# A two-layer decoder trunk: both layers in one unrolled program, four input tiles at a time

## The chip, the cores and the metric

The kernel runs on one core of one Trainium2 chip. The metric is the device time of one execution in microseconds (us); lower is better. Three runs of the kernel before gave 1854.80, 1850.37 and 1839.76 us, with a median of 1850.37 us. The engines are called PE (TensorE), ACT (ScalarE), DVE (VectorE), POOL (GpSimd) and SP (SyncE, which here only issues DMAs).

## The reference

A float32 decoder trunk with two layers, 512 tokens and a width of 1024. Cut to what matters here:

```python
for l in range(DEPTH):                       # DEPTH = 2
    h = rms_norm(x, norm_mix_pre[l])
    parts = jnp.split(h @ w_in[l], splits, axis=-1)
    # three head groups: latent attention (8 heads), mLSTM (4), dilated window attention (4)
    y = jnp.concatenate([y_a, y_b, y_c], axis=-1) @ w_out[l]
    x = x + rms_norm(y, norm_mix_post[l])
    h = rms_norm(x, norm_x_pre[l])           # cross-attention into 256 memory tokens
    y = memory_cross_attention(h, rms_norm(mem, norm_mem[l]), x_w_q[l], x_w_kv[l], x_w_o[l])
    x = x + rms_norm(y, norm_x_post[l])
    h = rms_norm(x, norm_ffn_pre[l])
    y = swiglu(h, w_gate_up[l], w_down[l])   # hidden width 2816
    x = x + rms_norm(y, norm_ffn_post[l])
```

## The kernel before

Everything is feature-major: `x` is 8 tiles of 128 features by 512 tokens and stays in SBUF. Each matrix product is split: operand and weight are each a high part (`h_hi`, `w_hi`) and a low remainder (`h_lo`, `w_lo`), and each 128 by 128 weight block costs three matmuls (lines 551 to 553, helper `three`).

**Weight stream.** The weights of a layer are 128 units of 512 KB, streamed in a fixed order through a ring of four slots (`RING`). For each unit SP loads `raw`, ACT copies it to `w_hi` (`split_unit`, line 852), POOL computes `w_lo` = raw - w_hi (`make_lo`, line 522), and PE uses both. SP may load a unit once the `w_lo` of the unit four before is made; ACT may write `w_hi` once PE has used the unit four before. POOL and SP walk through the units in hardware loops of four (`each_unit`).

**Layer loop.** The two layers are one hardware loop (line 488). Each turn is a block with one program for each engine, followed by a block that clears the semaphores, each with a meeting of all engines at its end. A block ahead of the loop loads `mem` (1 MB), the first gains, four weight units, `x` (2 MB) and the constants (1.7 MB), and makes the memory's `mem_rstd` (ACT square, 16 short matmuls at line 483, ACT Ln and Exp). The weights of units 0 to 3 come from a second array (`first_in`), and units 0 and 1 of the next layer are split ahead of the end of the loop's turn (`AHEAD` = 2). The last block stores `x` in one DMA of 2 MB (line 1499) and waits for it.

**Input stage** (lines 608 to 629 on PE). For each of the 8 k tiles of x, ACT makes `h_hi[k]` (`scaled_hi`) and the square `sq[k]` (two buffers), and DVE makes `h_lo[k]` (`scaled_lo`) and adds the square to `acc` (`add_square`). PE takes two output tiles side by side over k (m = 0 and 1, units 0 and 1), sums the squares over the partitions (`norm_sum`, line 596), and ACT turns the sum into `mix_rstd` (lines 873 and 875). Then come output tiles 2 to 9, one after the other, alternating between PSUM banks 0 and 1: tile m waits until tile m - 2 has been taken out by DVE (`take`, line 1134, multiplied by `mix_rstd`). After tile 7 PE waits for the squares of the query part (`norm_sum("q")`). `project_tokens` (96 matmuls, units 10 to 13) then fills banks 2 to 5 (`wide`), and the tile `sw` 0 follows. The 4-row matmuls at line 654 end the stage.

**DVE in that stage** (lines 1176 to 1242) has one fixed order: takes 0 to 9 in between the gates, four convolutions of four operations each (`convolve`), and four `silu` with a reciprocal of 3.35 us each. The take of tile 9 (`OG + 1`) stands at line 1224, ahead of the last `silu`, the norm of the query part and the taking out of the token-major banks.

**Residuals.** `residual` (line 1143) multiplies each y tile by `rstd` and adds it to x. After cross-attention and after the FFN, POOL adds tiles 1, 3, 4 and 6 (`POOL_ADDS`, line 528) and DVE the others; after cross-attention DVE makes `h_lo` and the square sums of the FFN's input in the same pass (`ffn_input`), and PE takes four gate/up tiles side by side over k.

## Time and profile before

| What | us |
|---|---|
| median of three runs | 1850.37 |
| lowest and highest run | 1839.76, 1854.80 |
| span of the profiled execution (first to last instruction) | 1837.1 |
| PE busy in it | 1674.5 (91%) |
| DVE busy | 1059.6 (58%) |
| ACT busy | 675.1 (37%) |
| POOL busy | 667.7 (36%) |

The span is taken in one profiled execution; the runs include what lies around it (the median is 13.3 us longer). Busy time of PE is modelled from pipelined matmuls, so a busy PE can still run below its peak; the column PEclk of a stretch is the TensorE clock that was granted (1.00 is 2.4 GHz, 0.50 is 1.2 GHz). A timeline row has its start, its length, engine, line and operation, and in brackets how long the engine was idle before it and what ended that.

### The profile page before, as it was taken

To read this page: it belongs to the slowest core of one execution; us is meant where nothing else is said; L and a number is where in the kernel's file an instruction comes from. 1 tells how busy PE (TensorE), PEld (TensorE's weight loads), DVE (VectorE), ACT (ScalarE), POOL (GpSimd) and SP (SyncE) were. 2 spreads that over 40 slices of the span, in tenths; PEclk is the share of its full clock that TensorE was granted. 3 is DMA by queue.
4 is the path that set the end of the run, shared out by engine and by line. 5 is a ranking of instruction groups with operands and counts; after the bars stand their busy time and mean duration, and the time that the engine had idled before them with its cause. 6 is when DMAs were issued, how large, how long until landed. Compare 5 with 4: busy or idle time off the path is not lost. (4 is left out here: it accounts for less than half of the span.)

```text
span 1837.1 us, 20577 instructions
## 1 busy us (share of the span) xinstructions
PE 1674.5 (91%) x7040; PEld 1267.2 (69%) x7040; DVE 1059.6 (58%) x1471; ACT 675.1 (37%) x1148; POOL 667.7 (36%) x280
## 2 busy tenths in 40 slices
PE   6998799989989999999769988998899899999994
PEld 4854456858667888888557545577677678888883
DVE  5977783661347786610279688727522587766003
ACT  5222574443442323322243226644343423232221
POOL 3321202563243444444333311035623345444442
PEclk9987899979989999999889889998999899999997
DMA  5211002332122232222122200023311132323231
GB/s 222 92 58 34 23 1 81 115 126 80 35 69 78 94 114 91 92 103 100 38 83 81 69 23 24 1 104 115 126 58 58 46 103 92 113 91 102 97 99 57
DMA packets 39100, 146.51 MB, mean 80 GB/s; under 512 B 4976, under 2 KB 4976, under 8 KB 38256
## 3 DMA queue, kind: packets, MB, share of 16 engines
q1 hardware_dynamic: 39024, 145.53, 23.4%
q8 instruction: 44, 0.72, 0.2%
q14 instruction: 32, 0.26, 0.0%
HBM read 143.41 MB, written 2.10 MB: 79 GB/s over the span
## 5 line engine op out<-in xcount | busy, mean ns | idle before, releaser
L522 POOL TENSOR_TENSOR w_lo<-raw,w_hi 128x1024 fp32r<-128x1024 f32 x252 | 620.6, 2469 | 1087.7 <-ACT w_hi L852 1087.6
L551 PE MATMUL bank<-h_hi,w_hi 128*128 128x512 f32 x1312 | 534.0, 407 | 69.8 <-DVE h_lo L1139 40.9
L552 PE MATMUL bank<-h_lo,w_hi 128*128 128x512 f32 x1312 | 520.0, 396 | 0.0
L553 PE MATMUL bank<-h_hi,w_lo 128*128 128x512 f32 x1312 | 519.6, 396 | 0.0
L551 PEld LDWEIGHTS bank<-h_hi,w_hi 128*128 128x128 f32 x1312 | 252.0, 192 | 144.2 <-issue 54.0
L852 ACT ACTIVATE w_hi<-raw 128x1024 fp32r<-128x1024 f32 x256 | 268.1, 1050 | 199.2 <-PE bank L553 199.0
L552 PEld LDWEIGHTS bank<-h_lo,w_hi 128*128 128x128 f32 x1312 | 252.4, 192 | 54.5 <-issue 3.2
L553 PEld LDWEIGHTS bank<-h_hi,w_lo 128*128 128x128 f32 x1312 | 251.9, 192 | 54.2
L1103 DVE TENSOR_TENSOR acc<-acc,sq 128x512 f32<-128x512 f32 x86 | 82.3, 956 | 321.7 <-ACT sq L864 320.0
L1455 DVE RECIPROCAL acc<-acc 128x512 f32<-128x512 f32 x44 | 147.5, 3353 | 1.5
L551 PE MATMUL bank<-a_hi,w_hi 128*128 128x512 f32 x352 | 138.7, 394 | 0.0
L553 PE MATMUL bank<-a_hi,w_lo 128*128 128x512 f32 x352 | 138.0, 392 | 0.0
L552 PE MATMUL bank<-a_lo,w_hi 128*128 128x512 f32 x352 | 136.6, 388 | 0.0
L1078 ACT ACTIVATE a_hi<-sq 128x512 f32 (+1 forms) x44 | 27.8, 632 | 253.2 <-DVE sq L1459 253.2
L864 ACT ACTIVATE sq<-bank 128x512 f32<-128x512 f32 x48 | 28.7, 598 | 147.0 <-PE bank L553 147.0
L553 PEld LDWEIGHTS bank<-a_hi,w_lo 128*128 128x128 f32 x352 | 66.1, 188 | 15.5
L552 PEld LDWEIGHTS bank<-a_lo,w_hi 128*128 128x128 f32 x352 | 66.1, 188 | 14.8
L551 PEld LDWEIGHTS bank<-a_hi,w_hi 128*128 128x128 f32 x352 | 66.2, 188 | 13.1
L1382 DVE CUSTOM_DVE_ANT_0 p_x<-bank,consts 128x256 f32<-128x256 f32 x32 | 13.6, 424 | 92.6 <-PE bank L783 91.6
L960 ACT ACTIVATE w_ml<-w_ml 128x512 f32<-128x512 f32 (+3 forms) x32 | 15.0, 470 | 135.6 <-DVE w_ml L1334 135.6
L1010 ACT ACTIVATE p_mix<-p_mix,stat 128x128 f32<-128x128 f32 (+1 forms) x96 | 53.6, 558 | 27.5 <-DVE stat L1382 27.4
L1382 DVE CUSTOM_DVE_ANT_0 p_mix<-bank,consts 128x128 f32<-128x128 f32 (+1 forms) x96 | 47.2, 491 | 21.2 <-PE bank L746 18.9
(184 smaller groups left out, 2212.8 us busy)
## 6 DMA issues: line engine op xcount, KB each, us to landing
raw<-w_in SPq DMA_DIRECT2D x248, 512.0 KB, 3.3
raw<-first_in SPq DMA_DIRECT2D x12, 512.0 KB, 3.5
mem<-mem_in SPq DMA_DIRECT2D x3, 1024.0 KB, 4.8
x<-x_in SPq DMA_DIRECT2D x1, 2048.0 KB, 10.6
out<-x SPq DMA_DIRECT2D x1, 2048.0 KB, 6.3
consts<-c_in SPq DMA_DIRECT2D x1, 1728.0 KB, 14.3
gains<-g_in SPq DMA_DIRECT2D x2, 36.0 KB, 4.1
first_g<-first_g_in SPq DMA_DIRECT2D x3, 4.0 KB, 3.3
```

The costliest lines, as they stand in the source:

```text
L522: pool.tensor_tensor(w_lo[:, s, :], raw[:, s, :], w_hi[:, s, :].bitcast(F32), ALU.subtract).then_inc(split_lo, 1)
L551: pe.matmul(out_ap, l_hi, r_hi, start=start, stop=False)
L552: pe.matmul(out_ap, l_hi, r_lo, start=False, stop=False)
L553: return pe.matmul(out_ap, l_lo, r_hi, start=False, stop=stop)
L852: act.activation(w_hi[:, s, :], raw[:, s, :], ACT.Copy)\
L864: act.activation(sq[:, c % 2, 0:width], src, ACT.Square).then_inc(squared, 1)
L960: act.activation(w_ml[:, u % 2, 0:n], w_ml[:, u % 2, 0:n], ACT.Exp).then_inc(ml_exp, 1)
L1010: act.activation(probs[:, u % PROBS, 0:n], probs[:, u % PROBS, 0:n], ACT.Exp, scale=-1.0, bias=stat[:, 0, u:u + 1], accum_out=stat[:, 1, u ...
L1078: act.activation(a_hi[:, bass.ds(j * (2 * SEQ) + i * SEQ, SEQ)], f_a[:, i, :], ACT.Copy)\
L1103: ins = dve.tensor_tensor(acc[:, :], acc[:, :], sq[:, s, :], ALU.add)
L1382: done(dve.tensor_tensor_reduce(probs[:, u % PROBS, 0:n], score_ring[u % 4][:, 0:n], const(mask(u // TB) + SEQ - n, n), -scale(u // TB), 3 ...
L1455: step(dve.reciprocal(e, e), 2)
```

## The change

- The layer loop, its barriers and the clearing of semaphores are gone: both layers are one unrolled program. Semaphores count on over both layers (`count`), waits are on constants; only the 10 turns of the gate/up loop stay hardware loops. SP and POOL are unrolled too.
- One weight array for 256 units; units 0 to 3 of the second layer are loaded and split as the ring gives room. All four are split before the second layer's input stage starts.
- At the start SP loads, in this order: unit 0, gains of both layers, x tiles 0 and 1, unit 1, x 2 and 3, unit 2, x 4 and 5, unit 3, x 6 and 7, constants. ACT splits unit k/2 ahead of x tile k. The memory's norm moves behind tile 5 of the first input stage; its data is loaded before unit 8.
- In the input stage PE takes four output tiles side by side over k (`HEAD` = 4); the ten output tiles go through banks 0 to 5 in turn (`IN_BANKS` = 6), and `project_tokens`, whose banks are 2 to 5, waits until DVE has taken out tile 9.
- The next layer's `h_hi`, `h_lo` and square sums are made inside the FFN's residual pass.
- All residual additions are on DVE.
- x is stored in four DMAs of 512 KB, each as soon as its two tiles are added.
- The memset of `ml_v` moves from before the first take to behind the query norm; the reload of `mem` is issued one unit earlier.

```diff
@@ sp, start and end
+                for s in range(RING):
+                    sp.dma_start(raw[:, s, :], w_in[s, :, :]).then_inc(raw_loaded[s], 16)
+                    if s == 0:
+                        sp.dma_start(gains[:, :, :], g_in).then_inc(gains_loaded, 16)
+                    sp.dma_start(x[:, 2 * s:2 * s + 2, :], x_in[:, 2 * s:2 * s + 2, :]).then_inc(x_loaded[s], 16)
+                sp.dma_start(consts[:, :], c_in).then_inc(consts_loaded, 16)
...
+                for i in range(KT // 2):
+                    sp.wait_ge(x_updated, count(x_updated, DEPTH - 1, N_SCALED - KT + 2 * i + 2))
+                    sp.dma_start(out[:, 2 * i:2 * i + 2, :], x[:, 2 * i:2 * i + 2, :]).then_inc(stored[i], 16)
@@ pe, project_step
-                        if k == 0 and use >= 2:
-                            wait_emptied(pe, use - 2)
+                        if name == "in" and k == 0 and m >= IN_BANKS:
+                            wait_emptied(pe, layer, use - IN_BANKS)
+                        if name != "in" and k == 0:
+                            wait_emptied(pe, layer, use - 2)
@@ pe, input stage
                     for k in range(KT):
                         after_norm("mix_pre")(k)
-                        for m in range(2):
+                        for m in range(HEAD):
                             project_step("in", m, k, tiles(h_hi), tiles(h_lo))
...
-                    for m in range(2, IN_FM):
+                    for m in range(HEAD, IN_FM):
                         project("in", m, tiles(h_hi), tiles(h_lo))
...
+                        if m == HEAD + 1 and layer == 0:
+
+                            pe.wait_ge(mem_squared, 1)
+                            pe.wait_ge(ln_done, 1)
+                            for k in range(KT):
+                                mm = pe.matmul(norm_bank[:, 0:N_MEM], const(C_ONES), mem_sq[:, k, :], start=(k == 0),
+                                               stop=(k == KT - 1))
+                            mm.then_inc(mem_summed, 1)
                         if m == ML[3]:
+                            if layer == 0:
+                                pe.wait_ge(mem_ln, 1)
                             norm_sum("q")
+                    wait_emptied(pe, layer, use_of("in", IN_FM - 1))
                     project_tokens(U_INV, wide, lambda k, b: h_hi[:, k, b * P:(b + 1) * P],
@@ act, before mix_rstd
                     for k in range(KT):
+                        if layer:
+                            wait_x(act, layer - 1, "ffn_post", k)
+                        elif k % 2 == 0:
+                            split_until(k // 2 + 1)
+                            act.wait_ge(x_loaded[k // 2], 16)
+                        scaled_hi(layer, k, G_MIX_PRE)
+                        square(layer, "mix_pre", k, x[:, k, :])
+                    split_until(HEAD + 1)
                     make_rstd("mix_pre", D_MODEL, mix_rstd)
@@ dve, residual and the end of the layer
-                                if name == "mix_post" or k - 1 not in POOL_ADDS:
-                                    dve.wait_ge(y_scaled, first + k)
-                                    done(dve.tensor_tensor(x[:, k - 1, :], x[:, k - 1, :], y[:, k - 1, :], ALU.add),
-                                         x_updated)
+                                dve.wait_ge(y_scaled, count(y_scaled, layer, first + k))
+                                done(dve.tensor_tensor(x[:, k - 1, :], x[:, k - 1, :], y[:, k - 1, :], ALU.add),
+                                     x_updated)
...
+                    def next_input(k):
+
+                        if k >= 1 and layer + 1 < DEPTH:
+                            scaled_lo(layer + 1, "mix_pre", k - 1, G_MIX_PRE)
+                            add_square(layer + 1, "mix_pre", k - 1)
+
+                    residual("ffn_post", "down", y_f, next_input)
+                    next_input(KT)
```

## Rows read from the trace of the kernel before

**Rows 1.** The page, parts 4 and 5: shares of the last chain; a costly group.

```profile
PE 36%; DVE 9%; issue 2%; ACT 1%; POOL 1%; DVEq 0%; POOLq 0%; ACTq 0%
...
L522 POOL TENSOR_TENSOR w_lo<-raw,w_hi 128x1024 fp32r<-128x1024 f32 x252 | 620.6, 2469 | 1087.7 <-ACT w_hi L852 1087.6
```

**Rows 2.** Busy time of each engine by stretch.

```profile
core 0: us, PE busy (x) PEld busy (x) DVE busy (x) ACT busy (x) POOL busy (x), PEclk, DMA share, GB/s
...
88.80:111.10 22.30, 22.30 (x98) 17.84 (x96) 17.82 (x19) 7.46 (x10) 10.94 (x4) 1.00 0.30 102
...
929.80:947.50 17.70, 14.17 (x50) 10.14 (x50) 15.57 (x17) 11.00 (x19) 5.69 (x2) 0.91 0.24 81
947.50:1000.90 53.40, 52.02 (x228) 42.02 (x229) 51.63 (x44) 17.49 (x24) 24.90 (x10) 1.00 0.28 94
```

**Rows 3.** Timeline, PE from layer 1 to layer 2 (start, length; idle before in brackets).

```profile
906.38 1.13 PE L596 MATMUL bank<-acc,consts 128*128 128x512 f32 x2 [1.48 <-DVE acc L1103]
...
929.84 0.79 PE L551 MATMUL bank<-h_hi,w_hi 128*128 128x512 f32 x1 [22.33 <-DVE h_lo L1139]
```

**Rows 4.** The page, part 6: DMA issues, count, KB each, us to landing.

```profile
raw<-w_in SPq DMA_DIRECT2D x248, 512.0 KB, 3.3
...
out<-x SPq DMA_DIRECT2D x1, 2048.0 KB, 6.3
consts<-c_in SPq DMA_DIRECT2D x1, 1728.0 KB, 14.3
```

**Rows 5.** Timeline, ACT, DVE and POOL as layer 1 starts.

```profile
23.15 1.04 ACT L852 ACTIVATE w_hi<-raw 128x1024 fp32r<-128x1024 f32 x1
...
24.10 0.71 ACT L884 ACTIVATE h_hi<-x,first_g 128x512 fp32r<-128x512 f32 x1
...
24.13 0.75 DVE L1139 SCALAR_TENSOR_TENSOR h_lo<-x,first_g,h_hi 128x512 fp32r<-128x512 f32 x1
...
24.27 2.86 POOL L522 TENSOR_TENSOR w_lo<-raw,w_hi 128x1024 fp32r<-128x1024 f32 x1 [10.98 <-ACT w_hi L852]
...
24.71 0.62 ACT L864 ACTIVATE sq<-x 128x512 f32<-128x512 f32 x1
...
24.92 2.77 DVE L1103 TENSOR_TENSOR acc<-acc,sq 128x512 f32<-128x512 f32 x1
```

**Rows 6.** Timeline, PE and DVE from cross-attention's residual into gate/up, layer 2.

```profile
1435.63 1.13 PE L596 MATMUL bank<-acc,consts 128*128 128x512 f32 x2 [1.48 <-DVE acc L1103]
1442.96 0.77 PE L551 MATMUL bank<-h_hi,w_hi 128*128 128x512 f32 x1 [6.20 <-DVE h_lo L1139]
...
1448.21 0.45 PE L551 MATMUL bank<-h_hi,w_hi 128*128 128x512 f32 x1
...
1456.02 0.69 DVE L1150 TENSOR_TENSOR y_x<-y_x,rstd 128x512 f32<-128x512 f32 x1
```

**Rows 7.** Timeline, layer 1: first input matmul, mix_rstd, end of the input stage.

```profile
17.72 0.50 PE L551 MATMUL bank<-h_hi,w_hi 128*128 128x512 f32 x1 [4.52 <-DVE h_lo L1139]
...
34.76 0.63 ACT L875 ACTIVATE mix_rstd<-mix_rstd 128x512 f32<-128x512 f32 x1
...
111.10 1.05 PE L654 MATMUL bank<-consts,gate 4*128 4x4 f32 x8
```

**Rows 8.** Timeline, input stage of layer 2: sum of squares, mix_rstd, DVE's chain.

```profile
945.03 1.10 PE L596 MATMUL bank<-acc,consts 128*128 128x512 f32 x2 [1.89 <-DVE acc L1103]
...
946.88 0.63 ACT L875 ACTIVATE mix_rstd<-mix_rstd 128x512 f32<-128x512 f32 x1
...
982.34 0.69 DVE L1103 TENSOR_TENSOR acc<-acc,sq 128x512 f32<-128x512 f32 x1
...
1000.24 0.69 DVE L1134 TENSOR_TENSOR o_gate<-bank,mix_rstd 128x512 f32<-128x512 f32 x1
```

**Rows 9.** Timeline, the end of the program.

```profile
1826.10 0.69 DVE L1155 TENSOR_TENSOR x<-x,y_f 128x512 f32<-128x512 f32 x1
1830.40 0.35 SPq L1499 DMA_DIRECT2D out<-x  x1
```

More of the change, by code:

```diff
@@ L224, in scaled_before @@
     return sum(k for n, k in NORMS[:NORM_AT[name]] if n in POST)
-def each_unit(eng, first, end, emit):
-    a, b = -(-first // RING) * RING, end // RING * RING
-    for n in range(first, min(a, end)):
-        emit(0, n)
-    if b > a:
-        with eng.Fori(a // RING, b // RING) as j:
-            for n in range(RING):
-                emit(j, n)
-    for n in range(max(a, b), end):
-        emit(0, n)
-def build(nc, x_in, mem_in, first_in, first_g_in, w_in, g_in, c_in, out):
+N_SQUARES = sum(k for _, k in NORMS)
@@ L280, in build @@
                 ml_qk = sb("ml_qk", [P, 4, SEQ], F32, early)
+                with ExitStack() as first:
+                    mem_sq = sb("mem_sq", [P, KT, N_MEM], F32, first)
                 ml_v = sb("ml_v", [P, TB, ML_HEADS, 2, ML_DK], F32, early)
@@ new lines, in _, with load @@
+                sp.dma_start(consts[:, :], c_in).then_inc(consts_loaded, 16)
+                def load(u):
+                    sp.wait_ge(split_lo, u + 1 - RING)
+                    sp.dma_start(raw[:, u % RING, :], w_in[u, :, :]).then_inc(raw_loaded[u % RING], 16)
+                for layer in range(DEPTH):
+                    first = layer * N_UNITS
+                    for n in range(0 if layer else RING, N_UNITS):
+                        if layer == 0 and n == 2 * RING:
+                            sp.dma_start(mem_sq[:, :, :], mem_in).then_inc(mem_first, 16)
+                        if n == U_OUT + RING + 1:
+                            sp.wait_ge(mix_at["out_lo"], count(mix_at["out_lo"], layer, MIX_HEADS))
+                            sp.dma_start(mem[:, :, :], mem_in).then_inc(mem_loaded, 16)
+                        load(first + n)
@@ L549, in three @@
+                pe.wait_ge(fixed_set, 2)
+                for layer in range(DEPTH):
                     def three(out_ap, l_hi, l_lo, r_hi, r_lo, start, stop):
@@ new lines, in _, with split_unit, split_to, scaled_hi @@
+            @block.scalar
+            def _(act):
+                done = counter(act)
+                act.preload_act_table_set("natural_log_exp_and_others")
+                made = [0]
+                def split_unit(layer, n, j=0):
+                    s = n % RING
+                    act.wait_ge(raw_loaded[s], j * 16 + count(raw_loaded[s], layer, 16 * (n // RING + 1)))
+                    if layer or n >= RING or not isinstance(j, int):
+                        act.wait_ge(unit_used, j * RING + count(unit_used, layer, n - RING + 1))
+                    act.activation(w_hi[:, s, :], raw[:, s, :], ACT.Copy).then_inc(split_hi, 1)
+                def split_to(layer, n):
+                    until = min(layer * N_UNITS + n, DEPTH * N_UNITS)
+                    while made[0] < until:
+                        split_unit(made[0] // N_UNITS, made[0] % N_UNITS)
+                        made[0] += 1
+                def scaled_hi(layer, k, g):
+                    act.activation(h_hi[:, k, :], x[:, k, :], ACT.Copy, scale=gains[:, layer, g + k:g + k + 1])\
+                       .then_inc(normed_hi, 1)
+                def square(layer, name, k, src, width=SEQ):
+                    c = layer * N_SQUARES + squares_before(name) + k
+                    if c >= 2:
+                        act.wait_ge(squares_added, c - 1)
+                    act.activation(sq[:, c % 2, 0:width], src, ACT.Square).then_inc(squared, 1)
+                for layer in range(DEPTH):
+                    def gain(col, rows=slice(0, P)):
+                        return gains[rows, layer, col:col + 1]
+                    def split_until(n):
+                        split_to(layer, n)
@@ L980, in _ @@
                         use = use_of("uk", m)
[L981 removed]
+                        wait_tile(act, layer, use)
                         for i in range(2):
@@ L1161, in tiles @@
                         return lambda k: t[:, k, :]
[L1164 to L1167 removed]
                     done(dve.memset(conv_in[:, :, 0:3], 0.0), pads_set)
[L1169 to L1171 removed]
+                    dve.wait_ge(rstd_ready, count(rstd_ready, layer, 1))
                     misc = c_tile(MISC)
```

598 lines of the change are left out of this document (248 added, 350 removed).

## Prediction

> **What bounds the kernel now.** I read the page's chain of waits first: PE has 36% of the chain that ended last, DVE 9% [rows 1], so PE is the bound where it has its operands and DVE where it hasn't. The table by stretch says where: in the token and `sw` part of the input stage PE is busy all 22.30 us with 98 matmuls, 0.2276 us each [rows 2]. That is PE's pace at full clock. Then I looked for places where PE has nothing: at the start (first input matmul at 17.72 [rows 7]), between the layers (idle for 22.33 us, ended by `h_lo` [rows 3]) and at the end (1826.79 to 1837.1). The change is aimed at these. Last I read DVE and POOL where PE is busy: in the 53.4 us behind the second layer's `mix_rstd` DVE is busy for 51.63 [rows 2]. PE and DVE are both full there, and the change ties them together anew.
>
> I call E the moment at which `mix_rstd` is ready: 34.76 + 0.63 = 35.39 in the first layer [rows 7], 946.88 + 0.63 = 947.51 in the second [rows 8]. The input stage ends at 111.10, 75.7 behind E [rows 7].
>
> **The store.** Before, the last addition ends at 1826.79, the store is issued at 1830.40 [rows 9] and takes 6.3 [rows 4]. After, DVE does eight scalings and eight additions of 0.69 each [rows 6, 9], about as long as now, when POOL's additions get in DVE's way. Only the last 512 KB lies behind them: a load of that size takes 3.3 [rows 4]. End: 1826.5 + 3.3 = 1829.8, that is **-7.3**. Bounds: a full 6.3 for the last piece, -4.3; 2.0 for it, -8.6.
>
> **Between the layers.** The new boundary has the form of the step from cross-attention to gate/up: residual with interleaved input, then four tiles over k. There PE's sum of squares starts at 1435.63, the first matmul at 1442.96, twelve matmuls run at half clock until 1448.21 (0.4375 each) [rows 6], and 84 at 0.2276 take 19.1: 1467.3. DVE needs 0.75 + 0.69 + 0.69 + 0.69 = 2.8 for each k [rows 5, 6, 9], PE 2.7, and DVE has a lead of 2.5, so DVE with all additions doesn't delay PE, here or after cross-attention, where I cost the moved additions at nothing. If that lead went, 8 x 0.1 is the price. From the sum's start to E it is 2.5 (945.03 to 947.51 [rows 8]): 1469.8, or 34.2 behind the start of the sum. After the FFN that sum starts at 906.38 [rows 3], so E = 940.6 instead of 947.5, **-6.9**. The fourth early split fits between two ACT operations; its `w_lo` falls on the first scaling, as it does after cross-attention. Bounds -5 and -9. Note how little 22 idle microseconds are worth: DVE needs four operations for each k where it had two passes, and PE does twice the matmuls before E.
>
> **The start of the first layer.** PE's first pass over m now needs four `w_lo` before it can go to k = 1. ACT splits in program order (w_hi 1.04, h_hi 0.71, sq 0.62; less where they overlap, 1.14 for a pair) [rows 5]; a `w_lo` is 2.4 on POOL alone (mean 2.469 [rows 1]). The row that matters is `acc` at 24.92: it took 2.77 instead of 0.69, because POOL worked from 24.27 to 27.13 [rows 5]; POOL in turn waited until `h_lo` ended at 24.88. So each `w_lo` stops DVE, and two square buffers make ACT wait for DVE. Worked out with the first landing at about 4 (0.7 + 3.3 [rows 4]) and the gains at 5.2:
> - w_hi 0 from 5.2 to 6.2, w_lo 0 to 8.7; h_lo 0 only then, to 9.3.
> - w_hi 1 behind k = 0 and 1, 8.4 to 9.5; w_lo 1 9.8 to 12.2; h_lo 1 and acc 1 to 13.6. sq 3 needs acc 1: 14.2.
> - w_hi 2 14.2 to 15.3; w_lo 2 15.9 to 18.3; acc 3 18.9. sq 5 needs acc 3: 19.5.
> - w_hi 3 19.5 to 20.6; w_lo 3 21.2 to 23.6.
>
> The DMAs aren't the gate: constants issued at 3.1 land at 17.4 behind 6.8 MB, and unit 3 is the first 3.7 MB [rows 4]. Behind PE's wait for w_lo 3 stand all matmuls of k = 1 to 7; ACT's split of unit 4 and `mix_rstd` wait for these. From 23.6 PE has 87 matmuls, 19.8, and 2.0 more at half clock: 45.4. With 2.5 more E = 48.0, **+12.6** though PE starts 8 us earlier. Bounds: with no blocking the chain is ACT's alone and w_lo 3 is ready at 18.5, +5.5 at full clock; with late gains and a slower first stretch, +15.
>
> The Trainium skill (SBUF — State Buffer, "Who interferes with whom" and the side section above it) says that the port pair of DVE and GpSimd is an exclusive lock held for a whole operation, not a split of bandwidth. By that rule the start costs the +12.6 above; were the pair shared, each `w_lo` would only stretch and the start would cost near +5.5. The trace agrees with the lock (2.77 for 0.69).
>
> **The input stage behind E.** Before, PE had tiles 2 to 9 left and its own banks for the tokens, so it never waited for the last takes. After, it has two tiles less to do, but `project_tokens` waits for take 9. That take ends at 1000.93, 53.4 behind E, and DVE had nearly no idle time before it: the chain of takes, convolutions and reciprocals is DVE's own and doesn't get shorter when PE is ahead. Behind PE's wait stand the tokens, the kv sum and `sw` 0, and DVE's taking out of the values and the mLSTM stage wait for those. Ten `w_lo` fall into it now (24.90 us of POOL [rows 2]), some eight after, since two are made earlier: I take 52.5. PE reaches `norm_sum("q")` at about E + 22 (E + 27 in the first layer, with the memory's norm) and waits for `acc`, ready at 983.03, E + 35.5 [rows 8]; tiles 8 and 9 with 12 slow matmuls take it to E + 50, within DVE's time. The tokens and `sw` 0 are 120 matmuls, 27.3, then the kv sum and the semaphore, 1.3: E + 81.1 instead of 75.7, **+5.4 in each layer**. The memory's norm in the first layer (5.4 of PE, 2.8 of ACT) lies in PE's wait for `acc` and costs nothing; without that cover 5.4. The `ml_v` memset (0.91) lies behind take 9 in DVE's slack while the tokens run. Bounds: 0 if DVE's blocking shrinks by 5, +8 if the tokens start at half clock.
>
> Barriers, clears and the first block are in the terms above. SP's earlier reload of `mem` meets a ring with three units made; 0.
>
> **Sum.** First layer +12.6 + 5.4 = +18.0; second -6.9 + 5.4 = -1.5; store -7.3: **+9.2**. Span 1837.1 + 9.2 = 1846.3, and the same added to the median, 1850.4 + 9.2 = 1859.6. I say 1859.
>
> **Rivals.**
> - *The new wait on take 9 doesn't bind.* DVE's chain is blocked less because PE's lead moves the `w_lo` under the reciprocals, which no row shows blocked. Then the term is 0 twice: +9.2 - 10.8 = -1.6, 1849. For: some 14 of the 53 us are blocking (the ten `w_lo` at 1.4 to 2.1 each, as the 2.08 of `acc` at the start [rows 5]). Against: the operations are the same, and ACT, which hands out the splits, still stops at the convolutions.
> - *Faster.* The same, and the start goes at ACT's pace (+5.5), and the chain shrinks until PE bounds it, -5 each: 5.5 - 10 - 6.9 - 7.3 = -18.7, 1832. It decides when take 9 ends before E + 43. The Trainium skill (Runtime: NRT & Kernel Launch, "Instruction fetch mechanics") says that a taken branch breaks the sequential fetch and that unrolling avoids this. By it this case would be likelier; but no row of POOL's idle time is ended by it, ACT's `w_hi` ends 1087.6 of 1087.7 [rows 1].
> - *Slower: the clock falls in the gap at `norm_sum("q")`* (8 to 14 us idle). If tiles 8 and 9 run wholly at half clock, 48 x 0.21 = 10 instead of 2.4 more, they end at E + 58, and the tokens start slow, +2.5. Against the sum each layer is 8.2 longer: +25.6, 1876. The gap before gate/up (6.20) cost twelve matmuls only, which speaks against; it decides from 4.7 more in each layer.
>
> **Chances.** Forecast 0.53 (own range 1851 to 1868), wait not binding 0.18, faster 0.09, slow clock 0.20. About 1% is what a measurement of this kernel can tell from no change: 1831.9 to 1868.9. The likeliest two lie inside; of the faster case most is just at the edge, of the slow case three quarters beyond, and of the forecast a little: faster 0.09, same 0.71, slower 0.20. The range leaves out the faster case and the far end of the slow one: 1840 to 1876.
>
> **What the changed profile would show.** The first four-tile round should complete not before 22, with `acc` or `h_lo` of 2.7 us beside each `w_lo`; E near 48 and near 958 (940.6 + 18.0 from the first layer); a wait of 8 to 14 us at the sum of the query squares and a wait of PE for DVE's take ahead of the tokens, which start 52 behind E; the sum after the FFN to the next E in 34; the last store 3.3 behind the last addition. I am wrong if the first round is complete by 18, if the tokens start before E + 48, or if the boundary takes longer than 37.

## The result and the profile after

The changed kernel takes 1847.78 us in the median (1844.44 to 1853.77, 20 runs) where the kernel before, in turn with it on the same chip, takes 1843.89 (1834.93 to 1854.80, 20 runs). The ratio is 1.0035, with a 95% interval from 1.0020 to 1.0049: 6.4 us more, 3.7 to 9.0 (the two medians alone differ by 3.9). A second comparison (`e14` below) gives 1.0027 [1.0012, 1.0041], 5.0 us more. The profiled execution has a span of 1851.4 us against 1837.1, that is 14.3 more; most of this section is about which part of the 14.3 is the change. Each run's time is 1.7 to 1.9 us above its own span, so the 13.3 us between span and median, which the section on the time before puts down to what lies around the span, are for the most part a difference between executions: a run of the kernel before with a span of 1837.1 has a time of 1838.9.

The page after, part 4 (the chain that ended last) and part 5 (costly groups: count, busy us, mean ns, idle before):

```profile
PE 75%; DVE 20%; ACT 2%; issue 1%; POOL 1%; DMA 0%; DVEq 0%; SPq 0%; ACTq 0%
...
L473 POOL TENSOR_TENSOR w_lo<-raw,w_hi 128x1024 fp32r<-128x1024 f32 x256 | 629.7, 2467 | 1178.3 <-ACT w_hi L804 1178.3
```

In [rows 1] the shares add up to 49%; here the chain is followed through the whole program, and PE and DVE hold 95% of it.

**The start.** Timeline of the changed kernel, PE, DVE, ACT and POOL (start, length; idle before in brackets):

```profile
8.72 0.76 PE L494 MATMUL bank<-h_hi,w_hi 128*128 128x512 f32 x1 [8.72 <-DVE h_lo L1092]
...
22.28 0.79 PE L494 MATMUL bank<-h_hi,w_hi 128*128 128x512 f32 x1 [4.92 <-POOL w_lo L473]
...
13.38 2.82 DVE L1086 TENSOR_TENSOR acc<-acc,sq 128x512 f32<-128x512 f32 x1
...
20.05 2.72 DVE L1086 TENSOR_TENSOR acc<-acc,sq 128x512 f32<-128x512 f32 x1
...
13.30 2.35 POOL L473 TENSOR_TENSOR w_lo<-raw,w_hi 128x1024 fp32r<-128x1024 f32 x1 [0.50 <-ACT w_hi L804]
19.40 2.82 POOL L473 TENSOR_TENSOR w_lo<-raw,w_hi 128x1024 fp32r<-128x1024 f32 x1 [3.75 <-ACT w_hi L804]
...
16.24 0.63 ACT L823 ACTIVATE sq<-x 128x512 f32<-128x512 f32 x1 [2.40 <-DVE acc L1086]
...
18.29 1.04 ACT L804 ACTIVATE w_hi<-raw 128x1024 fp32r<-128x1024 f32 x1
...
46.70 0.63 ACT L841 ACTIVATE mix_rstd<-mix_rstd 128x512 f32<-128x512 f32 x1
```

PE starts 9.0 us earlier than in [rows 7], and E (the moment at which `mix_rstd` is ready) comes 11.9 later (47.33 for 35.39). The fourth `w_lo` ends at 22.22, since POOL waited 3.75 us for ACT's `w_hi`, ACT's square had waited 2.40 for `acc`, and that `acc` took 2.82 instead of 0.69 beside the third `w_lo`.

**The input stage.** PE and DVE, first layer and then second:

```profile
84.17 2.04 PE L541 MATMUL bank<-acc,consts 128*128 128x512 f32 x2 [10.78 <-issue]
...
99.24 0.69 DVE L1137 TENSOR_TENSOR o_gate<-bank,mix_rstd 128x512 f32<-128x512 f32 x1
...
99.98 0.50 PE L494 MATMUL bank<-w_hi,h_hi 128*128 128x512 f32 x1 [1.17 <-DVE o_gate L1137]
...
993.70 2.08 PE L541 MATMUL bank<-acc,consts 128*128 128x512 f32 x2 [13.47 <-DVE acc L1086]
...
1009.23 0.50 PE L494 MATMUL bank<-w_hi,h_hi 128*128 128x512 f32 x1 [1.62 <-DVE o_gate L1137]
```

PE stands for 10.8 and 13.5 us at the sum of the query squares, and once more for the take of tile 9. The tokens start at E + 52.6 and E + 51.6 (before: 47.5 in both layers), and the stage ends at 128.29 and 1037.54, E + 81.0 and E + 79.9.

**Between the layers.** PE and ACT:

```profile
923.82 1.13 PE L541 MATMUL bank<-acc,consts 128*128 128x512 f32 x2 [1.48 <-DVE acc L1086]
...
930.89 0.77 PE L494 MATMUL bank<-h_hi,w_hi 128*128 128x512 f32 x1 [5.94 <-issue]
...
957.01 0.63 ACT L841 ACTIVATE mix_rstd<-mix_rstd 128x512 f32<-128x512 f32 x1
```

The 22.33 us of [rows 3] are 5.94, but from the sum to E it is 33.8 us where it was 41.1.

**The end.** The last two additions on DVE, and the DMA issues of the page's part 6:

```profile
1846.84 1.41 DVE L1150 TENSOR_TENSOR x<-x,y_f 128x512 f32<-128x512 f32 x2
...
out<-x SPq DMA_DIRECT2D x4, 512.0 KB, 2.6
```

The span ends at 1851.4, 3.1 behind the last addition; in [rows 9] it was 10.3.

**What a single profile hides.** The next table cuts the span of all profiled kernels at the sums of squares and at the matmuls that turn the gates. "Unchanged" is everything else: mLSTM, attention, cross-attention and FFN of both layers. There every kernel does the same work; what differs is that the unrolled kernels have no layer loop and no loops of units, that POOL or DVE makes four of the additions behind cross-attention, and where tensors lie.

| kernel | start to first sum | sum to gates, layer 1 | FFN's sum to next first sum | sum to gates, layer 2 | last sum to end | unchanged |
|---|---|---|---|---|---|---|
| before | 32.9 | 78.2 | 38.7 | 78.2 | 24.6 | 1584.5 |
| e6 (before, addresses) | 32.9 | 78.2 | 39.2 | 78.2 | 24.5 | 1597.9 |
| e13 (before, addresses) | 33.6 | 78.3 | 39.4 | 78.2 | 24.6 | 1585.0 |
| changed | 44.9 | 83.4 | 31.4 | 82.3 | 16.3 | 1593.1 |
| e14 (changed again) | 43.8 | 83.3 | 30.6 | 81.9 | 16.3 | 1591.9 |
| e4 (addresses, two more loads) | 46.5 | 83.6 | 31.5 | 82.3 | 16.3 | 1592.3 |
| e2 | 36.7 | 83.4 | 30.4 | 82.8 | 16.3 | 1585.4 |
| e1 | 27.1 | 86.6 | 30.7 | 81.9 | 16.3 | 1591.9 |
| e3 | 43.8 | 81.6 | 30.4 | 81.8 | 16.3 | 1587.1 |
| e10 | 44.8 | 79.6 | 30.6 | 79.8 | 16.3 | 1598.3 |
| e5 | 44.6 | 83.4 | 30.4 | 82.9 | 19.9 | 1586.3 |
| e8 (addresses) | 45.0 | 83.5 | 30.7 | 81.9 | 16.3 | 1585.1 |
| e7 | 26.3 | 81.2 | 25.5 | 78.0 | 16.3 | 1581.2 |
| e9 (e7, addresses) | 26.0 | 81.3 | 25.5 | 78.1 | 16.3 | 1590.9 |
| e11 (e7, addresses) | 26.9 | 81.2 | 25.5 | 78.1 | 16.3 | 1580.0 |
| e12 (e11, POOL adds) | 26.1 | 81.2 | 26.3 | 78.1 | 17.5 | 1576.9 |

The five changed stretches repeat within about 1 us in kernels that share their code. The unchanged ones don't: with the same code and the same addresses they took 1581 us (e7) to 1598 us (e10), at mean granted clocks of 0.968 and 0.953 in these stretches (0.966 and 0.948 over the whole execution). At equal clock the two programs can agree there to 0.1 us: from the gates to the next sum of squares, versions of the kernel before took 229.9, 233.2, 225.9 and 228.4 us at clocks of 0.911, 0.898, 0.917 and 0.918, and versions of the unrolled one 229.9, 233.1, 226.0 and 228.4 at the same four; other pairs with one mean clock still lie up to 2.9 us apart, in either program. Of the 14.3 us between the first two profiles, 8.5 lie in the unchanged part; 4.7 of them are the down projection (below), the rest is scatter of this kind. The changed stretches give +12.0 + 5.2 - 7.2 + 4.1 - 8.3 = +5.8 us for these two profiles; with means over three profiles of before and over the changed one, e14 and e8, it is +11.5 + 5.2 - 8.2 + 3.8 - 8.3 = +4.0.

### The profile page after: what moved, and what is told of

It is laid out like the page before. It is cut to its first block, busy times and chain, and to the rows that moved or that the text cites. A ratio compares the mean times of both kernels' runs of the same rounds, so it can differ in the third digit from the quotient of the medians.

```text
span 1851.4 us, 19318 instructions
## 1 busy us (share of the span) xinstructions
PE 1687.9 (91%) x7040; PEld 1273.8 (69%) x7040; DVE 1054.8 (57%) x1486; ACT 671.2 (36%) x1144; POOL 635.9 (34%) x262
## 4 chain that ended last, share of the span: by engine, by line
PE 75%; DVE 20%; ACT 2%; issue 1%; POOL 1%; DMA 0%; DVEq 0%; SPq 0%; ACTq 0%
PE bank L494 21%; PE bank L495 20%; PE bank L496 20%; PE bank L709 3%; PE bank L703 3%; PE bank L681 2%; DVE tn_x L1120 2%; DVE x L1150 2%; PE bank L750 2%; DVE y_x L1146 2%; PE bank L740 1%; DVE ml_qk L1174 1%; DVE conv_in L1183 1%; PE bank L633 1%; DVE o_gate L1297 1%
## 5 line engine op out<-in xcount | busy, mean ns | idle before, releaser
L473 POOL TENSOR_TENSOR w_lo<-raw,w_hi 128x1024 fp32r<-128x1024 f32 x256 | 629.7, 2467 | 1178.3 <-ACT w_hi L804 1178.3
L1086 DVE TENSOR_TENSOR acc<-acc,sq 128x512 f32<-128x512 f32 x86 | 74.7, 868 | 327.3 <-ACT sq L823 325.6
L1371 DVE CUSTOM_DVE_ANT_0 p_x<-bank,consts 128x256 f32<-128x256 f32 x32 | 13.6, 425 | 94.3 <-PE bank L740 93.3
```

The lines of the kernel that those rows point to most:

```text
L473: pool.tensor_tensor(w_lo[:, u % RING, :], raw[:, u % RING, :], w_hi[:, u % RING, :].bitcast(F32), ALU.subtract).then_inc(split_lo, 1)
L1086: ins = dve.tensor_tensor(acc[:, :], acc[:, :], sq[:, c % 2, :], ALU.add)
L1371: done(dve.tensor_tensor_reduce(probs[:, u % PROBS, 0:n], score_ring[u % 4][:, 0:n], const(mask(u // TB) + SEQ - n, n), -scale(u // TB), 3 ...
```

## The experiments

My theory was that of the prediction: the loss is the first layer's four tiles and the tokens' wait for the last take; the gains are the boundary and the store. The ratios below are to the kernel before on the same chip; "against the changed kernel" means against 1.0031, the mean of its two ratios, at 1841 us. Each ratio is uncertain by 0.15 to 0.3%, 3 to 6 us.

### Two tiles in the first layer (e1)

```diff
+        def head(layer):
+            return HEAD if layer else 2
-                        for m in range(HEAD):
+                        for m in range(head(layer)):
```

> The first layer takes two input tiles at a time over k again, the second layer still four. Theory (the first layer's loss lies in the first pass of PE over m, which needs four w_lo, each of them tied behind DVE and ACT): the first pair needs only the first two w_lo, complete at about 13 us, the pass over k then takes as long as before the change (17.7 us), mix_rstd is ready at 29 to 31 us instead of 47.3, the input stage ends at 110 to 113 instead of 128.3, and the kernel is 16 to 18 us faster than the changed kernel, 1830 to 1832. Rival A (cold unrolled code or the first weights' landing sets the start whatever the number of tiles): mix_rstd stays after 40, gain under 7. Rival B (the start is regained, but given back behind mix_rstd, since PE has two more tiles to do there): mix_rstd at 30 but the input stage ends after 118, gain under 10.

1833.16 us, ratio 0.9958 [0.9937, 0.9978]: 13 us faster than the changed kernel. ACT and PE of its first layer:

```profile
28.90 0.63 ACT L845 ACTIVATE mix_rstd<-mix_rstd 128x512 f32<-128x512 f32 x1
...
83.45 0.80 PE L498 MATMUL bank<-w_hi,h_hi 128*128 128x512 f32 x1 [5.89 <-DVE o_gate L1141]
...
113.72 1.05 PE L615 MATMUL bank<-consts,gate 4*128 4x4 f32 x8
```

E comes at 29.53, 17.8 earlier; the stage ends 14.6 earlier, at E + 84.2, because PE waits 5.9 us for the take of tile 9, which ends at E + 53.9. The theory holds for the start; 3 us go the way of rival B, and the gain of 13 us lies below the 16 to 18 expected.

### Weights ahead of x (e2)

```diff
-                            split_until(k // 2 + 1)
+                            split_until(RING)
```

and the loads of x stand behind those of the four units.

> The four first weight units are loaded ahead of x, and ACT rounds all four before it touches x; four tiles over k stay. Theory (the fourth w_lo is late because ACT rounds units 1 to 3 only between squares that wait for acc on DVE, which each w_lo on POOL stops): the fourth w_lo ends at 15 to 17 us instead of 22.2, mix_rstd is ready at 39 to 42 instead of 47.3, and the kernel is 5 to 8 us faster than the changed kernel. Rival (POOL's own work or the landing of the units is the bound): the fourth w_lo stays after 20 and the gain is under 2 us.

1838.99 us, ratio 0.9986 [0.9965, 1.0007]: 8 us faster than the changed kernel. POOL and ACT:

```profile
5.66 9.90 POOL L474 TENSOR_TENSOR w_lo<-raw,w_hi 128x1024 fp32r<-128x1024 f32 x4 [5.21 <-ACT w_hi L805]
...
38.52 0.63 ACT L842 ACTIVATE mix_rstd<-mix_rstd 128x512 f32<-128x512 f32 x1
```

The four `w_lo` are made in 9.9 us without a break (DVE's first operation beside them starts at 12.21, during the third) and end at 15.56, 6.7 earlier; E at 39.15 is 8.2 earlier. e2 moves the loads too, but these were not what made the fourth late: in the changed kernel unit 3 had landed at 13.68 us, and ACT came to split it at 18.29. It was the interlocking of ACT, POOL and DVE.

### The wait for the last take (e3, e10)

e3 puts tiles 8 and 9 into banks 0 and 1 and the query's sum behind tile 9; e10 keeps the sum, and after the first four tiles uses banks 0 and 1 only, as before the change:

```diff
-                    wait_emptied(pe, layer, use_of("in", IN_FM - 1))
+                    wait_emptied(pe, layer, use_of("in", HEAD - 1))
```

> Input tiles 8 and 9 go to the two banks of the later tiles, so that the six banks of the tokens are free once DVE has taken tile 5; the sum of the query squares moves behind tile 9. Theory (PE's wait for the take of tile 9 sets the input stage's end): the tokens start about E + 45 or earlier instead of E + 52.6, the stage ends at E + 73 to E + 76 instead of E + 81.0 and E + 79.9, and the kernel is 9 to 15 us faster than the changed kernel. Rival (DVE's chain is the bound anyway, and the mLSTM stage waits for DVE instead): the tokens start earlier, but the stage's end moves by under 2 us in each layer, and so does the kernel.

> The changed kernel, four tiles over k in banks 0 to 3, but the later tiles alternate in banks 0 and 1 as before the change, so that the tokens have banks 2 to 5 for themselves and don't wait for the take of tile 9; the sum of the query squares stays where it is. Theory (the wait on the last take makes the input stage longer, by its place in PE's order and not by DVE's chain): the tokens start between E + 46 and E + 49, the stage ends at E + 75.5 to E + 77.5 in both layers instead of E + 81.0 and E + 79.9, mix_rstd as in the changed kernel (47.3), and the kernel is 6 to 9 us faster than the changed kernel. Rival (DVE's chain of takes bounds it in any case, as with the sum moved): E + 79 or more, gain under 3.

e3 takes 1846.13 us, 1.0028 [1.0005, 1.0051]; e10 1846.08, 1.0021 [1.0002, 1.0041]. PE in the first layer of e3, then of e10:

```profile
83.72 0.80 PE L494 MATMUL bank<-h_hi,w_hi 128*128 128x512 f32 x1 [11.44 <-DVE q_mla L1136]
...
96.81 0.80 PE L494 MATMUL bank<-w_hi,h_hi 128*128 128x512 f32 x1
...
125.40 1.05 PE L610 MATMUL bank<-consts,gate 4*128 4x4 f32 x8
```

```profile
71.31 0.79 PE L494 MATMUL bank<-h_hi,w_hi 128*128 128x512 f32 x1 [5.86 <-DVE q_mla L1137]
...
96.13 0.39 PE L494 MATMUL bank<-w_hi,h_hi 128*128 128x512 f32 x1
...
124.31 1.05 PE L611 MATMUL bank<-consts,gate 4*128 4x4 f32 x8
```

In e3 (E = 46.22) the wait for take 9 is gone, but one of 11.4 us for take 6 (the `q_mla` of the row) stands in its place at tile 8, after it PE starts slowly (0.80 for a matmul), and the tokens start at E + 50.6. The stage ends at E + 79.2: 1.8 gained, 0.5 in the second layer. The expectation of 9 to 15 us was wrong. In e10 (E = 47.16) the waits come earlier and the tokens start at E + 49.0, the stage ends at E + 77.2 and E + 77.4, that is 3.8 and 2.5 earlier. Take 9 itself ends later in e10, at E + 54.4; it was the place of the wait in PE's order, and not DVE's chain, that cost these us. The stretches are as e10's theory had them, 6.3 us in sum; its gain of 6 to 9 us in the kernel's time is not shown: the ratio gives 2 with 3.6 of uncertainty, and this profile had the slowest unchanged part of all.

### One store at the end (e5)

```diff
-                for i in range(KT // 2):
-                    sp.wait_ge(x_updated, count(x_updated, DEPTH - 1, N_SCALED - KT + 2 * i + 2))
+                sp.wait_ge(x_updated, count(x_updated, DEPTH - 1, N_SCALED))
+                sp.dma_start(out, x[:, :, :]).then_inc(stored[0], 16)
```

> The four stores of 512 KB become one of 2 MB behind the last addition. Theory (the store's term of the prediction): the last DMA takes 6.3 us to landing instead of 2.6, so the kernel is 3.7 us slower than the changed kernel, 1851 to 1852. Rival (the pieces share the same queues and the last one is not faster for being small, or the end is set elsewhere): less than 1 us of difference.

1852.10 us, ratio 1.0055 [1.0034, 1.0076]: 4.4 slower than the changed kernel; the last stretch is 19.9 instead of 16.3. Part 6 of its page gives the one transfer as:

```profile
out<-x SPq DMA_DIRECT2D x1, 2048.0 KB, 6.3
```

### The input stage of the kernel before, in the changed program (e7)

```diff
-HEAD = 4
-IN_BANKS = 6
+HEAD = 2
+IN_BANKS = 2
-                    wait_emptied(pe, layer, use_of("in", IN_FM - 1))
```

and the first sum stands behind the last k of tile 0, as before the change.

> The changed kernel (one program without barriers, one weight stream, pieces of the store, additions on DVE) with the input stage of the kernel before: two tiles over k in both layers, two banks for the input tiles, and the tokens in banks of their own, without the wait for the last take. Theory (four tiles and six banks cost more than they give in both layers, the rest of the change gains): mix_rstd is ready at 29 to 31 us in the first layer and 30 to 34 behind the sum after the FFN in the second; each input stage ends 75 to 77 behind mix_rstd, instead of 81.0 and 79.9; the kernel is 21 to 27 us faster than the changed kernel, 1820 to 1826, and faster than before by over 0.8%. Rival (at the boundary four tiles are what hides DVE's four operations for each k): mix_rstd of the second layer comes no later than with four tiles only if PE catches up; if it comes over 37 behind the sum, the gain is that of the first layer alone, 14 to 18.

1816.49 us, ratio 0.9878 [0.9848, 0.9908]: 22 us faster than before and 28 faster than the changed kernel. Its chain, ACT at both E's, and the table by stretch for the boundary and the second input stage:

```profile
PE 77%; DVE 18%; ACT 2%; issue 1%; DMA 0%; POOL 0%; DVEq 0%; SPq 0%; ACTq 0%
```

```profile
28.16 0.63 ACT L841 ACTIVATE mix_rstd<-mix_rstd 128x512 f32<-128x512 f32 x1
...
925.35 0.63 ACT L841 ACTIVATE mix_rstd<-mix_rstd 128x512 f32<-128x512 f32 x1
```

```profile
core 0: us, PE busy (x) PEld busy (x) DVE busy (x) ACT busy (x) POOL busy (x), PEclk, DMA share, GB/s
...
898.00:926.00 28.00, 16.29 (x52) 9.98 (x52) 22.04 (x33) 13.28 (x22) 2.35 (x1) 0.88 0.07 20
926.00:1001.60 75.60, 74.38 (x325) 59.95 (x325) 70.37 (x64) 24.96 (x32) 36.20 (x14) 1.00 0.30 97
```

The boundary takes 28.0 us from the sum to E, though PE is busy for only 16.3 of it: DVE's pace for each k sets it, and two tiles are done by then. One `h_lo` follows the other after 2.84 us, and PE waits 1.2 of them for it. With four tiles, 96 matmuls in place of 48 stand ahead of E. The second stage takes 75.6, as before the change, and PE is busy for 74.4 of it: nothing is lost by doing the two tiles there. The first takes 78.7, 3.1 more than the second, where the memory's norm is missing: it now has no wait of PE to hide in (its matmuls run from 41.8 to 45.1). E and the boundary come slightly earlier than expected, and so the kernel is faster than the 1820 to 1826 asked for. Against the means of the kernel before the stretches of the table give -6.8 + 3.0 - 13.6 - 0.2 - 8.3 = -25.9, and the down projection +4.7: -21, where the ratio says 22 (17 to 28).

### The pace of the down projection (e4, e6, e8, e9, e11, e13)

The traces showed a difference that my sum doesn't contain. PE in the down projection, first and last of a run of back-to-back matmuls; before (36 of them), changed (36), e8 (37):

```profile
849.80 0.39 PE L551 MATMUL bank<-a_hi,w_hi 128*128 128x512 f32 x1
...
857.81 0.39 PE L553 MATMUL bank<-a_hi,w_lo 128*128 128x512 f32 x1
```

```profile
849.61 0.39 PE L495 MATMUL bank<-a_lo,w_hi 128*128 128x512 f32 x1
...
857.77 0.40 PE L494 MATMUL bank<-a_hi,w_hi 128*128 128x512 f32 x1
```

```profile
849.74 0.39 PE L496 MATMUL bank<-a_lo,w_hi 128*128 128x512 f32 x1
...
857.90 0.39 PE L496 MATMUL bank<-a_lo,w_hi 128*128 128x512 f32 x1
```

8.01 / 35 = 0.2289 us from start to start before, 8.16 / 35 = 0.2331 in the changed kernel, 8.16 / 36 = 0.2267 in e8, all at a granted clock of 1.00 and with no wait between them. The code is the same; what differs is where the tensors lie. The changed kernel has gains of 640 bytes for each partition where there were 320 in two tensors, and a `stat` of 576 bytes instead of 768. Over all 528 matmuls of a layer the first and the last start are 120.6 us apart before, 123.0 in the changed kernel and 119.5 in e8, the same in both layers. The edits move small tensors only (e4 also loads the gains in three pieces), for example in e8:

```diff
-        stat = sb("stat", [P, 3, MIX_UNITS])
+        stat = sb("stat", [P, 2, MIX_UNITS])
+        sb("gap", [P, 16])
```

> The changed kernel with the gains in three tensors, so that the weight ring, y_f, h_hi, h_lo and sq stand at the SBUF addresses that they have in the kernel before (in the changed kernel they lie 320 bytes higher); a_hi and a_lo stay at the changed kernel's addresses (128 bytes higher). Nothing else differs but two small loads more at the start. The matmuls of the down projection go at one each 0.2334 us in the changed kernel and 0.2289 in the one before. Theory A (the address of the ring does it): 0.2289 here, the FFN stage 1.1 to 3 us shorter in each layer, the kernel 2 to 5 us faster than the changed kernel. Theory B (the address of a_hi and a_lo, or something that is no address): 0.2333, no difference above 1 us.

> The kernel before, with 320 unused bytes behind the gains and 192 bytes less in stat, so that ring, h_hi, h_lo, a_hi and a_lo stand at the changed kernel's addresses; no instruction differs but in addresses. If SBUF addresses set the pace of the down projection, its matmuls go at 0.2333 us here instead of 0.2289, and the kernel is 2 to 5 us slower than before. If they don't (the unrolled program or its waits do), it is 0.2289 and within 1 us of before.

> The changed kernel with a_hi and a_lo 128 bytes lower, at the addresses that they have in the kernel before (stat keeps two rows instead of three, and the reciprocal overwrites the row of the maxima); ring, h_hi and h_lo stay where the changed kernel has them. Theory A, now that the ring alone didn't bring the pace back and the kernel before lost it with both moved: the address of a_hi and a_lo sets the pace of the down projection, so its matmuls go at 0.2289 us each instead of 0.2333, the stretch from the sum ahead of gate/up to the one behind down is 1.5 to 2.5 us shorter in each layer, and the kernel is 3 to 5 us faster than the changed kernel (1842 to 1845 where the kernel before takes 1841). Theory B (ring and a must both stand as before): 0.2333 and no gain.

> The version with two tiles and own banks (e7), all tensors from x on 32 bytes up and a_hi and a_lo 160 bytes down, so that ring, h_hi, h_lo, a_hi and a_lo begin at multiples of 64 bytes; before, in the changed kernel and in e7 they all begin 32 bytes beside one. If a multiple of 64 is what matmul's moving operand wants, down goes faster than 0.2289, gate/up faster than in e7, and the kernel is 5 us or more faster than e7 (under 1812). If only the distance of the address from something else counts, down goes at 0.2289 or 0.2333 and the kernel stays within 4 us of e7 (1812 to 1818).

> e7 (two tiles, own banks) with a_hi and a_lo left at the changed kernel's address, and ring, h_hi and h_lo 128 bytes up, so that the distance from the ring to a_hi is a multiple of 256 bytes, as it was in e8 (down at 0.2267 us each) and in none of the others (rest 64 in the kernel before: 0.2289; rest 128 in the changed kernel, 192 in the two others: 0.2333). Theory A (the distance between the weights and the moving operand, modulo 256 bytes, sets the pace): 0.2267, the stretch from the sum ahead of gate/up to the one behind down is 347.2 to 347.6 us in both layers instead of 350.9, and the kernel is 5 to 8 us faster than e7, 1809 to 1812. Theory B (the address of a_hi itself, 139104, is the good one): 0.2333 and no gain against e7.

> The kernel before with a_hi and a_lo 64 bytes lower (stat without its unused columns, 128 unused bytes behind it), so that their distance from the ring is a multiple of 256 bytes instead of a multiple and 64. Theory (the distance modulo 256 sets the pace): down at 0.2267 us for each matmul instead of 0.2289, the stretch from the sum ahead of gate/up to the one behind down at 346 to 347.4 us, and the kernel 1 to 3 us faster than before. Otherwise 0.2289 and within 1 us.

From the start of `raw` to `a_hi` it is the ring (49152 bytes), `h_hi` and `h_lo` (32768), `sq`, `acc`, `rstd`, `mem_rstd` (9216), `stat`, `acol` (64) and what was put between. `raw`, `w_hi` and `w_lo` lie 16384 bytes apart and `a_lo` 45056 behind `a_hi`, all multiples of 256, so that the rest is the same for each pair of weight and operand:

| kernel | `raw` to `a_hi`, bytes | its rest by 256 | down, us for each matmul | sum ahead of gate/up to sum behind down | ratio |
|---|---|---|---|---|---|
| before | 91968 | 64 | 0.2289 | 348.5, 347.2 | 1 |
| changed | 91776 | 128 | 0.2333 | 349.5, 349.5 | 1.0035 |
| e14 | 91776 | 128 | 0.2333 | 350.9, 350.9 | 1.0027 |
| e6 | 91776 | 128 | 0.2333 | 350.9, 350.9 | 1.0020 |
| e4 | 92096 | 192 | 0.2333 | 349.5, 349.5 | 1.0049 |
| e9 | 91584 | 192 | 0.2333 | 350.9, 349.5 | 0.9864 |
| e7 | 91776 | 128 | 0.2333 | 350.9, 350.9 | 0.9878 |
| e8 | 91648 | 0 | 0.2267 | 347.4, 347.4 | 0.9997 |
| e11 | 91648 | 0 | 0.2267 | 346.0, 346.0 | 0.9837 |
| e13 | 91904 | 0 | 0.2267 | 347.4, 347.3 | 0.9980 |

e1, e2, e3, e5 and e10 have the layout of the changed kernel and 0.2333, e12 that of e11 and 0.2267. The fifth column has two causes. Where the granted clock was 1.00 throughout, the stretch takes 346.0 us with a rest of 0, 347.2 with 64 and 349.5 with 128 or 192; where the record has one short fall to 0.50 in it, 1.3 to 1.4 us more (347.4, 348.5, 350.9).

Four readings fell on the way. The ring's address alone is not it (e4). `a_hi` at the address of before isn't what does it either: e8 has it there and goes at 0.2267, not at the 0.2289 of before, and e11 has it at the changed kernel's address and goes at 0.2267 too. Beginning at multiples of 64 bytes does nothing (e9; all others begin 32 beside one). And the unrolled program isn't it (e6 is the kernel before, and slow). The rest by 256 fits all ten rows, and in e11 and e13 it was named beforehand. Gate/up, whose operand `h_hi` lies 49152 bytes (a multiple of 256) above `raw`, goes at 0.2267 in every kernel. So the e8 expectation got its faster pace for another reason than it gave: it named the address of `a_hi` alone and asked for 0.2289. The weights were always moved together with `h_hi`, `h_lo` and `sq`, and ACT and POOL write in the ring while PE reads; which of these accesses meets which, no run separates. For 528 matmuls in each layer, 0.2333 instead of 0.2289 is 2.3 us, 4.7 in all; against 0.2267 it is 7.0. In time: e13 is 4 us faster than before [0.9965, 0.9995] and e6 4 slower [1.0001, 1.0039], both clear of no change by little. e8 is 6 us faster than the changed kernel, with about 4 of uncertainty; for e11 against e7 it is 8, with about 8, which the time alone doesn't show. The pace in the traces is what carries this section.

### Additions on POOL again (e12)

```diff
+POOL_ADDS = (1, 3, 4, 6)
-                                done(dve.tensor_tensor(x[:, k - 1, :], x[:, k - 1, :], y[:, k - 1, :], ALU.add),
-                                     x_updated)
+                                if name == "mix_post" or k - 1 not in POOL_ADDS:
```

> e11 with the additions 1, 3, 4 and 6 of the residuals behind cross-attention and the FFN on POOL again, as before the change. Prediction's step: DVE with all additions doesn't delay PE, so handing four of them back to POOL changes neither the stretch from the sum behind cross-attention to the one ahead of gate/up (29.2 to 29.5) nor that from the sum after the FFN to the next mix_rstd (27.9 in e7) by more than 0.5 us, and the kernel stays within 2 us of e11. Rival A (with two tiles at the boundary DVE's four operations for each k are the bound there): the boundary gets 1 to 3 us shorter. Rival B (POOL's additions stop DVE for longer than DVE needs for them): both stretches get 1 to 3 us longer.

1811.20 us, ratio 0.9839 [0.9806, 0.9873], against 1812.81 and 0.9837 [0.9803, 0.9870] for e11: no difference in time. In the stretches of one profile each the boundary is 26.3 instead of 25.5 and the end 17.5 instead of 16.3, the way of rival B. POOL and DVE at its end:

```profile
1794.66 0.68 DVE L1168 TENSOR_TENSOR y_f<-y_f,rstd 128x512 f32<-128x512 f32 x1
...
1799.96 1.64 POOL L491 TENSOR_TENSOR x<-x,y_f 128x512 f32<-128x512 f32 x1 [0.63 <-DVE y_f L1168]
...
1800.52 1.63 DVE L1168 TENSOR_TENSOR y_f<-y_f,rstd 128x512 f32<-128x512 f32 x1
```

DVE's scaling takes 1.63 instead of 0.68 beside POOL's addition. Where both have work, having the additions on DVE gains 0.8 us at the boundary and 1.2 at the end; behind cross-attention e12 took 28.9 and 29.6, e11 29.4 and 29.5.

### The changed kernel once more (e14)

> The changed kernel once more, nothing altered, beside the kernel before. If the stages changed are all there is: +5.8 us and 2.3 to 2.5 in each layer from the down projection, +10.5, a ratio of 1.0057. If the first measurement stands: 1.0035. An interval that holds one and not the other decides.

1845.28 us, ratio 1.0027 [1.0012, 1.0041]. It holds 1.0035 and not 1.0057. What the difference is comes below.

## Why the prediction came out as it did

The forecast said 1859 us, 9 above the median that was shown. It came to 1847.8: inside the range of 1840 to 1876, but 11 too high. Some 6.5 of the 11 are the base: the 20 runs of before beside the changed kernel have a median of 1843.9, where the three that the forecast started from had 1850.4. The rest is the change itself, +9.2 forecast, +6.4 and +5.0 by the ratios (+3.9 between the medians). That the time lies inside the range says little, since the 1843.9 of no change would lie in it too.

Point by point, with the terms of the sum:

- **Start of the first layer, +12.6 forecast.** +11.9 in the two profiles, 11.5 in the means. The mechanism is that of the prediction: `acc` at 2.82 and 2.72 beside `w_lo`, ACT's squares waiting for it, the fourth `w_lo` at 22.2 (forecast 23.6), and not before 22 as asked. e1 and e2 confirm it from two sides. PE starts at half pace there, as forecast: its matmuls start 0.43 us apart from 22.3 to 28.0 and 0.227 after.
- **Input stage behind E, +5.4 in each layer.** +5.3 and +4.2. Take 9 ends at E + 52.6 in the first layer (forecast 52.5) and E + 51.5 in the second. The waits at the query's sum are 10.8 and 13.5 (forecast 8 to 14). e10 gives 3.8 and 2.5 of it back, so the banks are the larger part. The remaining 1.5 and 1.7 are not taken apart.
- **Between the layers, -6.9.** -7.3 in the two profiles, -8.2 in the means: from the sum to E 33.8 us (forecast 34.2), 33.0 in most other profiles, while the kernel before takes 41.1 in one profile, 41.7 in e6 and 41.9 in e13. This gain was put too small.
- **The store, -7.3.** -8.3. The last 512 KB land in 2.6 (forecast 3.3), and DVE's sixteen operations take 13.2 from the last sum to the last addition instead of 14.3, since POOL's additions no longer stop it. The forecast had 0.3 for that (1826.79 to 1826.5); e12 gives it as 1.2.
- **The moved additions at nothing.** Right where PE is ahead (29.3 and 29.7 before, 29.5 twice after, behind cross-attention), a gain of about 1 at the boundary.
- **Down projection: missing.** The sum has no term for addresses. It is worth +4.7 by the trace and 3.7 [0.2, 7.2] by the time of e6.

The step that failed is therefore the sum and not a mechanism. All its terms were taken on the dear side: +9.2 together, where the same stretches show +5.8 in the two profiles and +4.0 in means. The most mis-sized are the input stage of the second layer (+5.4; +4.1 and +3.8 measured from sum to gates), the store (-7.3; -8.3) and, in means, the boundary (-6.9; -8.2). And the sum puts the down projection at nothing without a reason, where the traces show +4.7. The dear terms and the missing one nearly cancel, which is luck; the 6.5 of the base stay.

With the +4.7 the stretches give 8.7 to 10.5, and measured are 5.0 [2.2, 7.6] and 6.4 [3.7, 9.0]. The granted clock of the runs accounts for the difference, as far as an estimate can show it. The 20 runs of the changed kernel have a mean clock of 0.952 and e14's 12 have 0.953, the 23 of the kernel before beside e14 have 0.948. Straight lines of time against clock through these three sets stand at 1851.2, 1851.9 and 1840.1 us for a clock of 0.950: +11 to +12 at equal clock, nearly what the stretches say. That is a correlation over runs; why the changed kernel's were granted more is not known. A gain from the unrolled program in the unchanged stretches is not needed for the sum, and the pairs at equal clock above show none.

Of the rivals, "the wait doesn't bind" fell (PE waits 1.2 and 1.6 us for take 9), and "the clock falls at the query's sum" held in its condition and fell in its price. The granted clock was 0.50 from 76.0 to 89.7 us and 1.00 after it; from the sum's end to the wait for take 9, PE needed 12.6 us for the 48 matmuls of tiles 8 and 9 in the first layer (84.17 + 2.04 to 98.81) and 11.8 in the second, where full pace is 10.9 and the rival wanted some 10 more, and the tokens started at full pace. "Faster" fell too: the start was not at ACT's pace and take 9 was not done by E + 43. The view of the Trainium skill on unrolling (Runtime: NRT & Kernel Launch, "Instruction fetch mechanics") is neither confirmed nor refuted: the taken branch of the layer loop stood in the old boundary, together with its barriers, and no run parts the two. That of DVE's port (SBUF — State Buffer, "Who interferes with whom") agrees once more: DVE's 2.82 for 0.69 and 1.63 for 0.68 each end 0.55 us behind the end of POOL's operation beside them (15.65 and 1801.60).

What the prediction didn't ask is the question that matters most: what would each part be worth alone? It treated four tiles as part of the package and found the package near zero. e7 shows that the rest of the change gains 22 us (17 to 28), and that four tiles and six banks give back all of it and more. With the means of the changed kernel and e14 against e7 they cost 18.1 at the start, 2.1 and 4.1 in the two stages and 5.5 at the boundary, 29.8 together (28 by the ratios), and gain in none of the stretches.

## What to carry to other kernels

When a change moves work, look at which side of the next common wait it lands. Four tiles over k filled idle time of PE, but they put PE's work ahead of E, for which DVE and everything else wait, and took it from a stretch in which PE must wait for DVE once it has nothing else: in e7 PE is busy for 74.4 of 75.6 us there, in the changed kernel it stands for 13.5 at the sum of the query squares. Cost each part of a bundled change alone, since gains of 22 us can hide behind a loss of 28. And when the same matmuls go at another pace at full clock without a wait, compare the addresses of their operands before looking at the program: here 128 bytes in the place of two tensors were worth 7.0 us by the traces.

The fastest version is e11 (two tiles, own banks, unrolled, distance a multiple of 256): 1812.81 us, 0.9837 [0.9803, 0.9870] of the kernel before, 28 to 30 us faster than it. e12 is as fast.

## What the runs showed of the hardware

- The pace of a stream of matmuls with a moving operand of 512 columns depended on the distance in bytes of a partition between weights and moving operand: 0.2267 us where it is a multiple of 256, 0.2289 with a rest of 64, 0.2333 with rests of 128 and 192. Three distances have a rest of 0 (49152, 91648, 91904), one has 64, one 128 and two 192. Why this is so no run shows; all rows are at a granted clock of 1.00.
- The same instructions at the same addresses took 1581 to 1598 us in the unchanged parts, at mean granted clocks of 0.968 and 0.953 there. A single profile can't tell apart kernels of this kind that differ by 10 us; the stretches cut at fixed points can, to about 1 us, and where they scatter more the granted clock of the stretch says why: one short fall to 0.50 in the FFN is 1.3 to 1.4 us.
- A DVE operation with two inputs in SBUF ended only behind the POOL operation beside it: 2.82 us for 0.69, 1.63 for 0.68.
